# Two-layer mixture-of-experts transformer, float32: each piece of expert weights loaded, awaited and given back as two halves

## The chip, the core and the metric

The kernel runs on one core of a Trainium2 chip. The core has TensorE (PE, with PEld for its weight loads), VectorE (DVE), ScalarE (ACT), GpSimd (POOL) and SyncE (SP), which here only issues transfers, and 16 DMA engines that bring data from DRAM. The metric is the device time of the launch in microseconds; lower is better.

## The reference

The function is a stack of two models; the second one's layers (RWKV, long convolution, neighbourhood attention, convolutional FFN) aren't touched by the change. The first has two layers of gated MLP and attention, cross attention to a memory, and a mixture of experts over 512 tokens of width 1024:

```python
def expert_choice_moe(h, w_router, w_gate, w_up, w_down):
    cap = EC_FACTOR * s // N_EXPERTS            # 2 * 512 // 16 = 64 tokens for each expert
    logits = jnp.einsum('bsd,de->bse', h, w_router, preferred_element_type=jnp.float32)
    aff = jax.nn.softmax(logits, axis=-1)
    gates, idx = lax.top_k(aff.transpose(0, 2, 1), cap)
    xs = h[b_ix, idx]
    a = jnp.einsum('becd,edf->becf', xs, w_gate)      # w_gate, w_up, w_down: [2, 16, 1024, 1024]
    u = jnp.einsum('becd,edf->becf', xs, w_up)
    y = jnp.einsum('becf,efd->becd', jax.nn.silu(a) * u, w_down)
    y = y * gates[..., None].astype(y.dtype)
    return jnp.zeros_like(h).at[b_ix, idx].add(y)
```

## The kernel before

The program is a row of stages, one after the other; each starts when all engines have left the one before. All large weights pass through a ring (class `Ring`). They are cut on the host into pieces of 128 partitions x 4096 floats, 16 KB a partition and 2 MB in all, laid out in DRAM in the order of use. The ring has 2 slots of its own, 2 more during the first model, and 3 lent ones (`lent_weights`) during the experts: 7 slots in an experts stage.

Only SP moves pieces. `feed` walks through the list of pieces in order. For each it picks the slot whose last piece is the oldest, waits until the semaphore `weights_used` says that this piece has been used (line 94), and issues one transfer (line 95). The user calls `take` ahead of a piece, which waits for the slot's `weights_landed` semaphore, and `done` on its last instruction, which adds 1 to `weights_used`.

The change is in the stage that `Experts.run` builds. First the tokens are routed (softmax, largest 64 of each expert, places), with little work for TensorE. Then follows a loop over 16 experts with 6 pieces each: two of `w_gate`, two of `w_up`, two of `w_down`, each with 4 blocks of 128 rows by 1024 columns. Per expert TensorE runs, in this order: `project(GATE, 0)`, `spread_places`, `project(GATE, 1)`, `put_back(0)` of the expert before, `project(UP, 0)`, `put_back(1)`, `project(UP, 1)`, `put_back(2)`, `turn_hidden`, `put_back(3)`, `down(0)`, up to three `pick`s for the next group of 4 experts, `down(1)`. A `project` or `down` uses one piece in 8 matmuls (4 blocks, two halves of the columns); each counts twice in the trace, so a piece is x16 there. ACT and DVE wait on `weights_used` too, to know that a projection is complete (`piece(e, 1)`, `piece(e, 3)`, `piece(e, 5)`).

When the stage begins, 4 pieces are loaded, and SP at once fills the 3 lent slots. So 7 pieces of 96 are there before the first matmul of an expert, and 89 are refills: each waits until the piece 7 places before it has been used. Behind the last expert piece, `feed` goes on with `w_in` of the next layer.

Of the kernel before, what the change touches and what calls it, by code (L numbers as in the profile page):

```python
# [26 lines left out]
P = 128  # L27
T = 512
D = 1024
# [21 lines left out]
class Ring:  # L51


    def __init__(self, nc, ctx, pieces, slots, lent):
        tile = ctx.enter_context(nc.sbuf_tensor("weight_ring", [P, slots, KT * SLOT_COLS], F32))
        self.landed = [ctx.enter_context(nc.semaphore(f"weights_landed{i}")) for i in range(slots + lent)]
        self.used = ctx.enter_context(nc.semaphore("weights_used"))
        self.begun = ctx.enter_context(nc.semaphore("first_weights_landed"))
        self.pieces, self.own = pieces, slots
        self.tiles = [tile[:, i, :] for i in range(slots)] + [None] * lent  # L60
# [13 lines left out]
    def begin(self, sp, cols):  # L74

        src, n = self.pieces[0]
        to, src = (a.rearrange("p (k n) -> p k n", n=n)[:, :, cols] for a in (self.tiles[0][:, 0:src.shape[1]], src))
        if cols.start == 0:
            sp.dma_start(to, src).then_inc(self.begun, 16)
        else:  # L80
            sp.dma_start(to, src).then_inc(self.landed[0], 16)
            self.last[0], self.slot[0], self.fills[0], self.fill[0], self.issued = 0, 0, 1, 1, 1

    def feed(self, sp, n):

        self.fed += n
        while self.issued < len(self.pieces):
            i = self.issued
            s = min((s for s in range(len(self.tiles)) if i < self.until[s]), key=lambda s: self.last[s])
            if self.last[s] >= self.fed:  # L90
                break
            if self.last[s] >= 0:
                sp.wait_ge(self.used, self.last[s] + 1)
            src, _ = self.pieces[i]
            sp.dma_start(self.tiles[s][:, 0:src.shape[1]], src).then_inc(self.landed[s], 16)
            self.last[s], self.slot[i] = i, s
            self.fills[s] += 1
            self.fill[i] = self.fills[s]
            self.issued += 1
# [10 lines left out]

    def view(self, i):

        src, cols = self.pieces[i]
        return self.tiles[self.slot[i]][:, 0:src.shape[1]].rearrange("p (k n) -> p k n", n=cols)

    def done(self, ins):

        ins.then_inc(self.used, 1)

# [41 lines left out]
def col_pieces(flat, rows, cols, tall=KT * P, wide=SLOT_COLS):  # L161
# [3 lines left out]
    for _, h, _, n in piece_shapes(rows, cols, tall, wide):  # L165
        out.append((flat[at:at + h * n].rearrange("(p x) -> p x", p=P), n))
# [64 lines left out]
class Chain:  # L231
# [369 lines left out]
    def tensor(self, pe):  # L601
# [10 lines left out]
        def product(unit, ks, finish):  # L612
            job = unit.job

            def weights_here(m):
# [9 lines left out]
                if unit.ends_piece:  # L625
                    pe.wait_ge(self.ring.used, unit.piece + 1)
# [734 lines left out]
class Experts:  # L1361
# [80 lines left out]
    def run(self):  # L1442
# [4 lines left out]
        with ExitStack() as ctx:  # L1447
# [30 lines left out]
            piece = lambda e, j: first + 6 * e + j + 1  # L1478
# [18 lines left out]
            def _(pe):  # L1497
# [51 lines left out]
                def down(e, part):  # L1549
# [5 lines left out]
                    for k in range(4):  # L1555
                        for half in range(2):
# [76 lines left out]
            def _(act):  # L1633
# [11 lines left out]
                for e in range(NE):  # L1645
# [3 lines left out]
                    act.wait_ge(ring.used, piece(e, 1))  # L1649
# [3 lines left out]
                    act.wait_ge(ring.used, piece(e, 5))  # L1653
# [3 lines left out]
            def _(dve):  # L1657
# [74 lines left out]
                for e in range(NE):  # L1732
# [10 lines left out]
                    dve.wait_ge(ring.used, piece(e, 3))  # L1743
# [1454 lines left out]
def weight_pieces(dram):  # L3198

    out = []  # L3200
    for l in range(2):
# [5 lines left out]
        for e in range(N_EXPERTS):  # L3207
            for w in ("w_gate", "w_up", "w_down"):
                out += col_pieces(dram[w][l, e], D, D, tall=D // 2, wide=D)
# [183 lines left out]
```

## Time and profile before

| | us |
|---|---|
| median of 3 runs | 3629.76 (3628.56 to 3632.1) |
| profiled execution, its time | 3630.33 |
| profiled execution, its span | 3629.0 |
| TensorE busy | 3366.4, 93% of the span |
| VectorE busy | 1816.6, 50% |
| ScalarE busy | 1110.0, 31% |
| bytes read from DRAM | 589.91 MB, 163 GB/s over the span |
| mean granted TensorE clock | 0.965 |

The two experts stages lie at about 437 to 931 and 1362 to 1858 us. A busy TensorE is a modelled figure; what matters for the change is which engine waits for which inside those stages, and when in them.

### The profile page before, as it was taken

Reading aid. Unit: us, or ns where it says so; the run is one execution under the profiler, and the core shown is the slowest. Engines: PE = TensorE matmul, PEld = TensorE weight load, DVE = VectorE, ACT = ScalarE, POOL = GpSimd, SP = SyncE. Lnnn points to the kernel's source line nnn. Section 1 sums busy time; section 2 is a strip of 40 time slices with the busy share of each in tenths; the row PEclk is TensorE's granted clock in tenths of the full one; section 3 lists DMA queues with packets and bytes.
Section 4 is the critical chain, followed back from the end, with each engine's and each line's share of the span. In section 5 each row is a group of like instructions: output and inputs, shape, how many; then the busy total and the mean of one; then the engine's idle time right before and its main releaser. Section 6 shows DMA issues by size and latency. Waiting matters only on the chain. (4 is left out here: it accounts for less than half of the span.)

```text
span 3629.0 us, 55850 instructions
## 1 busy us (share of the span) xinstructions
PE 3366.4 (93%) x23850; PEld 2342.4 (65%) x23850; DVE 1816.6 (50%) x2872; ACT 1110.0 (31%) x1871; POOL 252.6 (7%) x208
## 2 busy tenths in 40 slices
PE   8889789999888997999989788889999999899999
PEld 7587543333667753333358687857888878688887
DVE  3655433222466443222245666566665462766635
ACT  3543300000345331000032333224333432643323
POOL 1011000000101100000020222201000110010001
PEclk9899999999989998999999899999999999999999
DMA  5031379999402217999952000012222222122222
GB/s 219 13 116 70 117 308 428 427 427 428 194 36 94 93 47 294 427 427 428 428 236 105 2 3 3 3 36 91 101 93 87 99 93 82 59 100 93 93 84 79
DMA packets 51798, 595.59 MB, mean 164 GB/s; under 512 B 5472, under 2 KB 9824, under 8 KB 16224
## 3 DMA queue, kind: packets, MB, share of 16 engines
q1 hardware_dynamic: 51552, 592.03, 40.5%
q8 instruction: 189, 3.10, 0.3%
q14 instruction: 57, 0.47, 0.0%
HBM read 589.91 MB, written 2.10 MB: 163 GB/s over the span
## 5 line engine op out<-in xcount | busy, mean ns | idle before, releaser
L648 PE MATMUL psum<-source_hi,weights_hi 128*128 128x512 f32 (+1 forms) x2352 | 921.4, 392 | 43.9 <-DVE weights_lo L535 35.7
L648 PE MATMUL psum<-source_lo,weights_hi 128*128 128x512 f32 (+1 forms) x2352 | 910.3, 387 | 0.0
L648 PE MATMUL psum<-source_hi,weights_lo 128*128 128x512 f32 (+1 forms) x2352 | 910.1, 387 | 0.0
L648 PEld LDWEIGHTS psum<-source_hi,weights_hi 128*128 128x128 f32 x2352 | 448.7, 191 | 144.7 <-DVE weights_lo L535 44.5
L648 PEld LDWEIGHTS psum<-source_lo,weights_hi 128*128 128x128 f32 x2352 | 448.8, 191 | 89.8 <-issue 2.9
L648 PEld LDWEIGHTS psum<-source_hi,weights_lo 128*128 128x128 f32 x2352 | 448.1, 191 | 88.8
L535 DVE TENSOR_TENSOR weights_lo<-weight_ring,weights_hi 128x1024 fp32r<-128x1024 f32 (+4 forms) x304 | 340.7, 1126 | 302.0 <-ACT weights_hi L483 301.3
L483 ACT CAST weights_hi<-weight_ring 128x1024 fp32r<-128x1024 f32 (+4 forms) x304 | 289.6, 960 | 660.2 <-PE psum L648 649.4
L1690 DVE TENSOR_TENSOR x<-psum,x 128x512 f32<-128x512 f32 x256 | 164.3, 685 | 199.7 <-PE psum L1571 199.7
L597 POOL TENSOR_TENSOR sums_of_squares<-squares 128x512 f32<-128x512 f32 (+1 forms) x17 | 27.2, 1598 | 2524.4 <-ACT squares L503 2524.4
L1538 PE MATMUL psum<-lent_weights,branches 128*64 128x512 f32 x800 | 182.1, 597 | 2.5 <-DMA lent_weights<-in_w_gate 2.5
L1538 PE MATMUL psum<-weight_ring,branches 128*64 128x512 f32 x624 | 141.8, 597 | 2.5 <-DMA weight_ring<-in_w_up 1.9
L1538 PE MATMUL psum<-weight_ring_first,branches 128*64 128x512 f32 x624 | 141.8, 597 | 2.5 <-DMA weight_ring_first<-in_w_up 2.3
L1538 PEld LDWEIGHTS psum<-lent_weights,branches 128*64 128x64 f32 x800 | 54.0, 137 | 114.6 <-issue 110.4
L597 POOL TENSOR_TENSOR sums_of_squares<-sums_of_squares,squares 128x512 f32<-128x512 f32 (+1 forms) x86 | 118.7, 1380 | 133.0 <-ACT squares L503 127.8
L2505 DVE TENSOR_TENSOR before_convolution<-psum,roots 128x512 f32<-128x512 f32 x100 | 69.0, 690 | 109.1 <-PE psum L648 109.0
L648 PE MATMUL psum<-weights_hi,source_hi 128*128 128x256 f32 x384 | 110.6, 288 | 11.7 <-DVE weights_lo L535 11.7
L2177 PE MATMUL psum<-rwkv_scratch 64*64 64x64 f32 x3584 | 108.2, 218 | 9.2 <-PEq L138 6.9
L2177 PEld LDWEIGHTS psum<-rwkv_scratch 64*64 64x64 f32 x3584 | 106.2, 135 | 15.0 <-issue 10.4
L1557 PE MATMUL psum<-lent_weights,hidden_t 128*64 128x512 f32 x480 | 109.1, 598 | 2.8 <-ACT hidden_t L1652 1.3
L1136 DVE TENSOR_TENSOR x<-psum,x 128x512 f32<-128x512 f32 x64 | 44.2, 691 | 132.8 <-PE psum L648 132.6
L1652 ACT COPY hidden_t<-psum 128x512 f32<-128x512 f32 x32 | 18.8, 587 | 298.9 <-PE psum L1546 298.9
(380 smaller groups left out, 4661.9 us busy)
## 6 DMA issues: line engine op xcount, KB each, us to landing
lent_weights<-in_w_down SPq DMA_DIRECT2D x30, 2048.0 KB, 17.9
lent_weights<-in_w_gate SPq DMA_DIRECT2D x26, 2048.0 KB, 16.6
lent_weights<-in_w_up SPq DMA_DIRECT2D x24, 2048.0 KB, 18.8
weight_ring<-in_ffn_w_up SPq DMA_DIRECT2D x22, 2048.0 KB, 7.7
weight_ring<-in_w_up SPq DMA_DIRECT2D x20, 2048.0 KB, 17.6
weight_ring_first<-in_w_up SPq DMA_DIRECT2D x20, 2048.0 KB, 17.3
weight_ring_first<-in_w_gate SPq DMA_DIRECT2D x19, 2048.0 KB, 16.5
weight_ring<-in_w_gate SPq DMA_DIRECT2D x19, 2048.0 KB, 16.5
```

Source lines behind the costliest of these rows:

```text
L483: act.copy(self.whi[:, ks, unit.slot * P:unit.slot * P + unit.cols], self.ring.view(unit.piece)[:, ks, unit.c0:unit.c0 + unit.cols])\
L535: ins = dve.tensor_tensor(lo, self.ring.view(unit.piece)[:, ks, unit.c0:unit.c0 + unit.cols], hi.bitcast(F32), ALU.subtract)
L597: pool.tensor_tensor(total, square(q) if m == 1 else total, square(q + m), ALU.add).then_inc(self.added, 1)
L648: ins = pe.matmul(ps, a, b, start=k == 0 and q == 0, stop=k == job.rows // P - 1 and q == 2)
L1136: return dict(evac=lambda i, dve, ps, link, r: dve.tensor_tensor(K.x[:, i, :], ps, K.x[:, i, :], ALU.add), engine=lambda i: "dve")
L1538: ins = pe.matmul(psum[HALF * half:HALF * half + HALF, which, :], self.xs[:, k, e // GROUP % 2, e % GROUP * CAP:(e % GROUP + 1) * CAP], w[ ...
L1557: ins = pe.matmul(psum[HALF * half:HALF * half + HALF, self.ROWS, :], hid_t[:, k, part * HALF:(part + 1) * HALF], w[:, k, half * 512:half ...
L1652: act.copy(hid_t[:, :, :], psum[:, self.TURN, :].rearrange("p (j s) -> p j s", j=4)).then_inc(hid_t_kept, 1)
L1690: dve.tensor_tensor(x, psum[:, bank(), :], x, ALU.add).then_inc(misc_free, 1)
L2177: ins = pe.matmul(K.psum[r, bank + d, c], w[d][r, lhs, c], w[d][r, rhs, c], start=True, stop=True)
L2505: return dve.tensor_tensor(self.raw[:, m % 3, :], ps, r[0], ALU.mult)
```

## The change

Every expert piece is marked with `ExpertPiece(True)`. SP moves such a piece as two transfers: the first two of its four blocks (8 KB of each partition's 16 KB), then the other two. The first half has the old semaphore `weights_landed`, the second a new one, `second_half_landed`. The first transfer waits only until the first half of the slot's old piece has been used, the second until all of it has. TensorE calls `done` after the fourth of a piece's 8 matmuls as well as after the last, and waits for the second half after the fourth. `weights_used` thus counts 2 for an expert piece and 1 for any other, and `releases[i]` is its value when piece i is used up; ACT, DVE and the other stages wait for these values at the same places in the work as before. Pieces of other weights are moved whole.

```diff
@@ Ring.__init__
+        self.second_landed = [ctx.enter_context(nc.semaphore(f"second_half_landed{i}")) for i in range(slots + lent)]
+        self.releases, n = [], 0
+        for _, _, experts in pieces:
+            n += 2 if experts else 1
+            self.releases.append(n)
@@ Ring.feed
-            if self.last[s] >= 0:
-                sp.wait_ge(self.used, self.last[s] + 1)
-            src, _ = self.pieces[i]
-            sp.dma_start(self.tiles[s][:, 0:src.shape[1]], src).then_inc(self.landed[s], 16)
+            src, _, experts = self.pieces[i]
+            old = self.last[s]
+            if experts and experts.in_halves:
+                half = src.shape[1] // 2
+                if old >= 0:
+                    sp.wait_ge(self.used, self.releases[old] - 1 if self.pieces[old][2] else self.releases[old])
+                sp.dma_start(self.tiles[s][:, 0:half], src[:, 0:half]).then_inc(self.landed[s], 16)
+                if old >= 0:
+                    sp.wait_ge(self.used, self.releases[old])
+                sp.dma_start(self.tiles[s][:, half:2 * half], src[:, half:2 * half]).then_inc(self.second_landed[s], 16)
+                self.second_fills[s] += 1
+                self.second_fill[i] = self.second_fills[s]
+            else:
+                if old >= 0:
+                    sp.wait_ge(self.used, self.releases[old])
+                sp.dma_start(self.tiles[s][:, 0:src.shape[1]], src).then_inc(self.landed[s], 16)
@@ Ring
+    def take_second_half(self, eng):
+        i = self.taken - 1
+        if i in self.second_fill:
+            eng.wait_ge(self.second_landed[self.slot[i]], 16 * self.second_fill[i])
@@ Experts.run
-            piece = lambda e, j: first + 6 * e + j + 1
+            used_up = lambda e, j: ring.releases[first + 6 * e + j]
@@ project
                     for k in range(4 * part, 4 * part + 4):
+                        if k % 4 == 2:
+                            ring.done(ins)
+                            ring.take_second_half(pe)
@@ down
                     for k in range(4):
+                        if k == 2:
+                            ring.done(ins)
+                            ring.take_second_half(pe)
```

On SP, the place is the start of the stage's refills; each row is one transfer with its shape, and `weights_used` is what TensorE raises. Before:

```order
50 L95 DMA weight_ring_first<-in_w_gate 128x4096 [waits weights_used]
51 L95 DMA weight_ring_first<-in_w_up 128x4096 [waits weights_used]
52 L95 DMA weight_ring<-in_w_up 128x4096 [waits weights_used]
53 L95 DMA weight_ring<-in_w_down 128x4096 [waits weights_used]
54 L95 DMA lent_weights<-in_w_down 128x4096 [waits weights_used]
```

With the change:

```order
60 L106 DMA weight_ring_first<-in_w_gate 128x2048 [waits weights_used]
61 L109 DMA weight_ring_first<-in_w_gate 128x2048 [waits weights_used]
62 L106 DMA weight_ring_first<-in_w_up 128x2048 [waits weights_used]
63 L109 DMA weight_ring_first<-in_w_up 128x2048 [waits weights_used]
64 L106 DMA weight_ring<-in_w_up 128x2048 [waits weights_used]
65 L109 DMA weight_ring<-in_w_up 128x2048 [waits weights_used]
```

Each transfer has become two, each behind a wait of its own; their order and their slots are the same.

On TensorE, the place is the first two pieces of the first expert, with the spread of the places between them. Before:

```order
1730 L1538 MATMUL psum<-weight_ring_first,branches 64x512 [waits weights_landed2,misc_free]
1731 L1538 MATMUL psum<-weight_ring_first,branches 64x512 x7
1732 L1530 MATMUL psum<-place_rows,constants 128x512 [waits misc_free]
1733 L1538 MATMUL psum<-weight_ring_first,branches 64x512 [waits weights_landed3]
1734 L1538 MATMUL psum<-weight_ring_first,branches 64x512 x7
```

With the change:

```order
1730 L1574 MATMUL psum<-weight_ring_first,branches 64x512 [waits weights_landed2,misc_free]
1731 L1574 MATMUL psum<-weight_ring_first,branches 64x512 x3
1732 L1574 MATMUL psum<-weight_ring_first,branches 64x512 [waits second_half_landed2]
1733 L1574 MATMUL psum<-weight_ring_first,branches 64x512 x3
1734 L1563 MATMUL psum<-place_rows,constants 128x512 [waits misc_free]
1735 L1574 MATMUL psum<-weight_ring_first,branches 64x512 [waits weights_landed3]
1736 L1574 MATMUL psum<-weight_ring_first,branches 64x512 x3
1737 L1574 MATMUL psum<-weight_ring_first,branches 64x512 [waits second_half_landed3]
```

The matmuls are the same and in the same order; a wait for the second half now stands ahead of the fifth of each piece's eight.

## Rows read from the trace of the kernel before

**Rows 1.** The page, part 2: GB/s of the DMA engines in 40 equal slices
```profile
GB/s 219 13 116 70 117 308 428 427 427 428 194 36 94 93 47 294 427 427 428 428 236 105 2 3 3 3 36 91 101 93 87 99 93 82 59 100 93 93 84 79
```

**Rows 2.** Windows in layer 0's experts; last three columns: clock, DMA share, GB/s
```profile
455.00:477.00 22.00, 15.70 (x149) 12.96 (x149) 9.89 (x21) 0.00 (x0) 0.00 (x0) 0.75 0.00 1
700.00:800.00 100.00, 99.18 (x482) 36.99 (x480) 29.95 (x50) 6.86 (x11) 0.00 (x0) 1.00 1.01 427
```

**Rows 3.** Waits of PE for DMA, 437 to 940: us in total, times, longest
```profile
PE psum L1538 <- DMA weight_ring<-in_w_up: 1.3, 3, 0.6
...
PE psum L1538 <- DMA weight_ring_first<-in_w_gate: 0.2, 1, 0.2
```

**Rows 4.** Timeline of PE, end of layer 0's experts: start us, us, engine, what
```profile
875.23 3.65 PE L1538 MATMUL psum<-weight_ring,branches 128*64 128x512 f32 x16 [0.15 <-DMA weight_ring<-in_w_up]
...
894.84 3.65 PE L1538 MATMUL psum<-lent_weights,branches 128*64 128x512 f32 x16 [1.23 <-DMA lent_weights<-in_w_gate]
899.74 3.65 PE L1538 MATMUL psum<-weight_ring_first,branches 128*64 128x512 f32 x16 [0.19 <-DMA weight_ring_first<-in_w_gate]
...
919.76 3.65 PE L1557 MATMUL psum<-lent_weights,hidden_t 128*64 128x512 f32 x16 [0.66 <-DMA lent_weights<-in_w_down]
```

**Rows 5.** Timeline of PE and SP, start of layer 0's experts: start us, us
```profile
473.38 3.63 PE L1538 MATMUL psum<-weight_ring_first,branches 128*64 128x512 f32 x16
...
477.06 0.33 SPq L95 DMA_DIRECT2D weight_ring_first<-in_w_gate  x1
481.69 0.33 SPq L95 DMA_DIRECT2D weight_ring_first<-in_w_up  x1
```

**Rows 6.** Timeline of PE's weight loads at a piece boundary
```profile
642.24 0.14 PEld L1557 LDWEIGHTS psum<-weight_ring_first,hidden_t 128*64 128x64 f32 x2 [0.29 <-issue]
642.67 0.14 PEld L1538 LDWEIGHTS psum<-weight_ring_first,branches 128*64 128x64 f32 x2 [0.29 <-issue]
```

**Rows 7.** DMA issues at 477.06, 481.69 and 883.86: KB each, us to landing
```profile
weight_ring_first<-in_w_gate SPq DMA_DIRECT2D x1, 2048.0 KB, 7.6
...
weight_ring_first<-in_w_up SPq DMA_DIRECT2D x1, 2048.0 KB, 9.3
...
weight_ring<-in_w_down SPq DMA_DIRECT2D x1, 2048.0 KB, 31.0
```

**Rows 8.** Timeline of ACT where the next stage begins
```profile
931.90 0.39 ACT L483 CAST weights_hi<-weight_ring_first 128x256 fp32r<-128x256 f32 x1
```

**Rows 9.** SP's issues (start us, us) and landings, 2048 KB then 1024 KB
```profile
913.23 6.24 SPq L95 DMA_DIRECT2D weight_ring<-in_w_in  x2
...
weight_ring<-in_w_in SPq DMA_DIRECT2D x1, 2048.0 KB, 21.2
...
weight_ring<-in_w_in SPq DMA_DIRECT2D x1, 1024.0 KB, 17.7
...
9.31 0.91 SPq L95 DMA_DIRECT2D weight_ring_first<-in_w_in  x2
...
weight_ring_first<-in_w_in SPq DMA_DIRECT2D x1, 2048.0 KB, 18.4
...
weight_ring_first<-in_w_in SPq DMA_DIRECT2D x1, 1024.0 KB, 20.5
```

**Rows 10.** SP's first issues, then their landings (x first, x last, w_in)
```profile
3.13 3.40 SPq L3162 DMA_DIRECT2D x<-in_x  x7
...
5.88 0.65 SPq L3162 DMA_DIRECT2D x<-in_x  x1
...
6.57 0.57 SPq L81 DMA_DIRECT2D weight_ring<-in_w_in  x1
...
x<-in_x SPq DMA_DIRECT2D x1, 256.0 KB, 5.0
...
x<-in_x SPq DMA_DIRECT2D x1, 256.0 KB, 6.3
...
weight_ring<-in_w_in SPq DMA_DIRECT2D x1, 1536.0 KB, 9.8
```

More of the change, by code:

```diff
@@ L12 @@
 import math
+from dataclasses import dataclass
 from contextlib import ExitStack, contextmanager
@@ L58, in __init__ @@
         self.begun = ctx.enter_context(nc.semaphore("first_weights_landed"))
+        self.second_landed = [ctx.enter_context(nc.semaphore(f"second_half_landed{i}")) for i in range(slots + lent)]
         self.pieces, self.own = pieces, slots
+        self.releases, n = [], 0
+        for _, _, experts in pieces:
+            n += 2 if experts else 1
+            self.releases.append(n)
+        self.second_fills = [0] * (slots + lent)
+        self.second_fill = {}
         self.tiles = [tile[:, i, :] for i in range(slots)] + [None] * lent
@@ L74, in begin @@
     def begin(self, sp, cols):
-        src, n = self.pieces[0]
+        src, n, _ = self.pieces[0]
         to, src = (a.rearrange("p (k n) -> p k n", n=n)[:, :, cols] for a in (self.tiles[0][:, 0:src.shape[1]], src))
@@ L109, in take @@
         return self.view(i)
+    def take_second_half(self, eng):
+        i = self.taken - 1
+        if i in self.second_fill:
+            eng.wait_ge(self.second_landed[self.slot[i]], 16 * self.second_fill[i])
     def view(self, i):
-        src, cols = self.pieces[i]
+        src, cols, _ = self.pieces[i]
         return self.tiles[self.slot[i]][:, 0:src.shape[1]].rearrange("p (k n) -> p k n", n=cols)
@@ L118, in done @@
         ins.then_inc(self.used, 1)
+@dataclass
+class ExpertPiece:
+    in_halves: bool
 class Core:
@@ L165, in col_pieces @@
     for _, h, _, n in piece_shapes(rows, cols, tall, wide):
-        out.append((flat[at:at + h * n].rearrange("(p x) -> p x", p=P), n))
+        out.append((flat[at:at + h * n].rearrange("(p x) -> p x", p=P), n, None))
         at += h * n
@@ L625, in weights_here @@
                 if unit.ends_piece:
-                    pe.wait_ge(self.ring.used, unit.piece + 1)
+                    pe.wait_ge(self.ring.used, self.ring.releases[unit.piece])
                 else:
@@ L1648, in _ @@
                         act.wait_ge(misc_free, scaled[c])
-                    act.wait_ge(ring.used, piece(e, 1))
+                    act.wait_ge(ring.used, used_up(e, 1))
                     act.activation(gated[:, :], psum[:, self.GATE, :], ACT.Silu, scale=column(e, 0)).then_inc(gate_kept, 1)
@@ L1652, in _ @@
                     act.copy(hid_t[:, :, :], psum[:, self.TURN, :].rearrange("p (j s) -> p j s", j=4)).then_inc(hid_t_kept, 1)
-                    act.wait_ge(ring.used, piece(e, 5))
+                    act.wait_ge(ring.used, used_up(e, 5))
                     act.copy(y_hi[:, :], psum[:, self.ROWS, :]).then_inc(y_hi_kept, 1)
@@ L1742, in _ @@
                     dve.wait_ge(gate_kept, e + 1)
-                    dve.wait_ge(ring.used, piece(e, 3))
+                    dve.wait_ge(ring.used, used_up(e, 3))
                     dve.scalar_tensor_tensor(out=hid[:, :], in0=psum[:, self.UP, :], scalar=column(e, 1), in1=gated[:, :],
@@ L3207, in weight_pieces @@
         for e in range(N_EXPERTS):
-            for w in ("w_gate", "w_up", "w_down"):
-                out += col_pieces(dram[w][l, e], D, D, tall=D // 2, wide=D)
+            six = [p for w in ("w_gate", "w_up", "w_down") for p in col_pieces(dram[w][l, e], D, D, tall=D // 2, wide=D)]
+            out += [(src, n, ExpertPiece(True)) for i, (src, n, _) in enumerate(six)]
     first, out = out, []
```

## The prediction, made before the change was run

> **What bounds the kernel now.** I read the page first: its slices of DMA have two plateaus near 428 GB/s [rows 1]. Those are the experts of the two layers, and the change touches nothing else. So I cut layer 0's stage into windows [rows 2] and take layer 1, whose plateau looks the same, to be alike. From 455 to 477 us the DMA engines idle: the ring's 7 slots are full, and TensorE releases none while the tokens are routed. In mid-stage DMA stands at 1.01 with TensorE at 99%.
>
> With both near full, the question is which of them sets the end. The list of waits answers: TensorE waits for weights only 4.2 us in the whole stage of layer 0, in five rows of which the first and the last stand here [rows 3]. In order of time [rows 4] all of it lies at the end. The first such wait is before the piece at 875.23; later pieces start at 894.84 and 899.74, 4.90 us apart, each behind its transfer, after matmuls of 3.65 us and a wait. So TensorE consumes a little faster than DMA delivers, lives on the 7 pieces' lead for 400 us, and has used it up at 875. From there the transfers decide, and since DMA has run full since the refills began [rows 1, 2], the end is: start of the refill stream, plus 89 pieces' transfers, plus TensorE's work behind the last landing.
>
> **The sum.** Three terms for each layer.
>
> Start. The first refill is issued at 477.06, when the first piece's last matmul has ended [rows 5]. The piece began at 473.38 [rows 5]. Weight loads come in steps of 0.43 us [rows 6], two records a step and 16 a piece, so half a piece is four steps, 1.72 us. The first half's slot is given back that much earlier, and an idle DMA can begin on it. Half a transfer (some 2.45 us) then covers the time to the second release. Gain 1.72. The later early releases gain nothing: late in the stage a transfer lands 31.0 us after its issue [rows 7], so six pieces queue in front of DMA, and a shorter time in a slot only lengthens the queue.
>
> End. The last piece starts at 919.76, when it has landed, and all that follows hangs on it, up to the next stage's first weights, cast at 931.90 [rows 4, 8]. With halves, the first four steps run while the second half is still arriving (2.45 us of transfer against 1.72 of work), and only 1.72 remains behind the landing. Gain 1.72. TensorE is free in time for this: it was idle 0.66 us before that piece. Together 3.44 a layer, less than the 4.2 that the waits hold, so TensorE's own work does not cap it.
>
> The transfers. What lands stays the same in bytes, but 128 rows of 16 KB become 256 rows of 8 KB, each half a strided read. The trace has no queue of such halves in this stage. It does have 1024 KB transfers behind 2048 KB ones: the one issued at 919.14 lands 2.41 us after its predecessor (919.14 + 17.7 less 913.23 + 21.2), the one issued at 9.79 lands 2.58 after (9.79 + 20.5 less 9.31 + 18.4) [rows 9]. Twice that is 4.82 to 5.16 against 4.90: from nothing to 0.26 us a piece. Shorter rows narrow it. Seven x tiles of 128 rows x 2 KB land between 3.13 + 5.0 and 5.88 + 6.3, six steps of 0.675 us, 84 ns for each of an engine's eight rows [rows 10]. At the expert rate (4.90 us for eight rows of 16 KB, 612 ns each) 2 KB would take 77, so a row costs 8 ns beyond its bytes. The transfer of 1536 KB in rows of 1536 B that skip 512 B each lands 4.19 us after the last x tile (6.57 + 9.8 less 12.18), 65 ns for each of 64 rows where bytes alone make 57: again 8 ns, so skipping in DRAM adds nothing [rows 10]. Eight more rows an engine make 0.064 us a piece. I take 0.05, a little under it, because the later of the two 1024 KB steps, the one in the same full stream, shows none. Over the 88 landings behind the first that is 4.4 us a layer.
>
> The Trainium skill, page "DMA: Bandwidth & Descriptors", section "Why small descriptors are slow (HBM only)", puts the overhead at some three cycles a packet; by the 32-byte beats of that section a piece in halves would take 0.6% longer, an estimate of 0.03 us, and the sum would come out at -1.9 us for both layers. The rows' 8 ns decide here.
>
> At nothing I put the rest. SP issues 192 more transfers, 0.33 us each [rows 5]: two in 4.90 us, and SP has nothing else queued. The waiting half on SP holds back only the next piece's request, which stands behind six queued pieces anyway. On TensorE each piece gets one more wait and one more signal. The boundary between two pieces without work between them has both already, and the 0.43 us step runs through it, from 642.24 to 642.67 [rows 6]; its upper bound is then 0.02 us a piece, 2 us a layer, hidden behind DMA's lead as long as it stays under the 4.2 us. ACT and DVE wait for the same end of the same pieces. w_in's third piece lands at 913.23 + 21.2 = 934.4, so its first, two transfers earlier, at 924.6, and that is first cast at 931.90 [rows 8, 9]: 7.3 us of cover, of which the net delay takes less than 3.
>
> Sum: (4.4 - 3.44) x 2 = +1.9 us on the profiled execution's 3630.3, 3632.2. That execution lies 0.6 over the median of the runs, so 3631.6 for the median. The change does what it says, and the engine that would profit was not short of lead until the end.
>
> **The rivals.** A measurement of this kernel can tell about 0.2%, 7.3 us, from no change.
>
> *The stream keeps its rate and starts better.* For it: the step of 2.41 us. The row cost would then be zero, and -3.44 x 2 = -6.9. In addition the second refill lands 6.3 us behind the first (481.69 + 9.3 less 477.06 + 7.6) where 4.90 are due [rows 5, 7]: DMA loses 1.4 us as it wakes. If half-size requests spare that too in both layers, the sum is -9.7, 3621. Against it: the wake-up is likely paid by the first packets whatever their size. It needs both parts to pass 7.3. Chance 0.12.
>
> *Halves cost more than rows say (slower).* Place: every landing from 484 to 920. It turns the sum over 7.3 us when a piece takes 0.080 us longer: 88 x 0.080 = 7.1 less 3.44, twice. At the upper row bound, 0.26, the sum is (22.9 - 3.44) x 2 = +38.9, 3669. For it: the step of 2.58 us, and that no row shows a long queue of halves. Against it: the 8 ns a row, which two row lengths, contiguous and not, give alike. Chance 0.17.
>
> The section "Anatomy of one DMA — SWDGE (gpsimd) path" of the Trainium skill's page "DMA: Bandwidth & Descriptors" gives each transfer a fixed 2 us next to its bytes. Here the row shows 4.90 us from landing to landing against 7.6 for the first, which found the queue empty [rows 7], so a fixed part exists and is hidden by the queue.
>
> *The fixed part is not hidden for halves.* If the 2.7 us between 7.6 and 4.90 stood between landings even in part, a tenth of it would give 88 x 0.27 = 23.8 less 3.44 a layer, +40.6 in all, 3671. Nothing in the rows shows it. Chance 0.03.
>
> *The extra waits on TensorE break its stream.* If a wait cost 0.1 us, 96 of them outweigh the 4.2 us of slack: TensorE would bound, about +9.6 - 4.2 = +5.4 a layer, 3641. Against it: the boundary in [rows 6]. Chance 0.05.
>
> **How the numbers follow.** The forecast and its near variants, row costs of 0 to 0.08 us a piece without a spared wake-up, run from -6.9 to +7.2 us, all within 0.2%: 0.63. Faster: 0.12. Slower: 0.17 + 0.03 + 0.05 = 0.25. The range leaves out the unlikely part of the first rival and the upper part of the second: from 3623 (no row cost, 3630 - 6.9) to 3645 (0.12 us a piece, (10.6 - 3.44) x 2 = +14.3), which holds about 0.85.
>
> **What the profile after would show.** The first refill issued near 475.3 instead of 477.1. 1024 KB transfers that land every 2.45 to 2.50 us in a DMA share of 1.00 to 1.01, and a rate of 423 to 425 GB/s where it was 427. The stage's first wait for DMA some 50 to 100 us earlier than 875, more and smaller waits in sum, half of them at the middle of pieces. 1.7 us from the last landing to the end of the matmuls. The rest of the kernel unchanged. I am wrong if the rate falls under 420 GB/s, if the weight loads' 0.43 us step breaks in the middle of pieces before 700, or if the wake-up loss is gone.

## The result, and the profile after

The median was 3628.32 us before and 3633.60 us after, 20 runs each (3622.5 to 3638.13, and 3631.13 to 3639.23). The ratio is 1.0016 with a 95% interval of 1.0010 to 1.0022: the change costs 5.8 us (3.6 to 8.0). That is a real loss and a small one, under the 0.2% (7.3 us) from which the prediction counts a kernel as slower. The prediction was 3631.6 us in a range of 3623 to 3645, and a loss of 1.9 us.

The profiled execution took 3631.13 us, its span 3629.7. First the page, part 2, as in [rows 1]:

```profile
GB/s 219 13 116 70 117 312 421 421 421 421 215 35 94 93 47 300 421 421 421 421 248 96 19 4 3 4 36 78 109 98 88 99 93 82 58 100 93 93 84 79
```

Both plateaus fell from 427 or 428 to 421 GB/s. They still are plateaus: the windows answering to [rows 2] show full DMA engines and a full TensorE.

```profile
455.00:477.00 22.00, 16.09 (x150) 13.11 (x150) 9.51 (x21) 0.00 (x0) 0.00 (x0) 0.76 0.06 13
700.00:800.00 100.00, 99.18 (x480) 36.98 (x478) 30.47 (x51) 6.85 (x11) 0.00 (x0) 1.00 1.01 421
```

So the DMA engines are as busy as before (1.01) and move less. Next the start of layer 0's experts, the timeline of TensorE and SP and the landings of these three transfers, as in [rows 5] and [rows 7]:

```profile
472.90 3.63 PE L1574 MATMUL psum<-weight_ring_first,branches 128*64 128x512 f32 x16
...
474.85 0.33 SPq L106 DMA_DIRECT2D weight_ring_first<-in_w_gate  x1
476.57 0.33 SPq L109 DMA_DIRECT2D weight_ring_first<-in_w_gate  x1
479.49 0.33 SPq L106 DMA_DIRECT2D weight_ring_first<-in_w_up  x1
...
weight_ring_first<-in_w_gate SPq DMA_DIRECT2D x1, 1024.0 KB, 4.9
...
weight_ring_first<-in_w_gate SPq DMA_DIRECT2D x1, 1024.0 KB, 6.7
...
weight_ring_first<-in_w_up SPq DMA_DIRECT2D x1, 1024.0 KB, 7.8
```

The first refill now starts 1.95 us after the first expert matmul (474.85 less 472.90), where it was 3.68: the stream starts 1.73 us earlier. But the first half lands at 479.75, the second at 483.27 and the third at 487.29, steps of 3.5 and 4.0 where a full stream makes 2.5.

The stage's end, on TensorE, as in [rows 4]:

```profile
866.69 1.94 PE L1574 MATMUL psum<-weight_ring_first,branches 128*64 128x512 f32 x8 [0.54 <-DMA weight_ring_first<-in_w_gate]
...
915.21 1.94 PE L1574 MATMUL psum<-weight_ring,branches 128*64 128x512 f32 x8 [0.49 <-DMA weight_ring<-in_w_up]
...
919.41 3.65 PE L1596 MATMUL psum<-weight_ring,hidden_t 128*64 128x512 f32 x16
922.89 1.89 PE L1596 MATMUL psum<-lent_weights,hidden_t 128*64 128x512 f32 x8
925.13 1.94 PE L1596 MATMUL psum<-lent_weights,hidden_t 128*64 128x512 f32 x8 [0.35 <-DMA lent_weights<-in_w_down]
```

A piece is now x8 and x8 wherever TensorE stopped in its middle. The last wait ends at 925.13, and 1.94 us of matmuls are left behind it, where a whole piece of 3.65 was left before. The first wait for DMA comes at 866.69 instead of 875.23. All waits of TensorE for DMA in the stage, the groups that answer to [rows 3]:

```profile
PE psum L1574 <- DMA weight_ring<-in_w_up: 2.8, 3, 1.8
...
PE psum L1574 <- DMA lent_weights<-in_w_gate: 1.1, 2, 0.6
PE psum L1574 <- DMA weight_ring_first<-in_w_gate: 1.1, 2, 0.6
PE psum L1596 <- DMA lent_weights<-in_w_down: 0.7, 2, 0.4
...
PE psum L1574 <- DMA weight_ring_first<-in_w_up: 0.5, 1, 0.5
```

They sum to 6.2 us in ten waits, where the five rows before summed to 4.2.

From the first expert matmul to the end of the last, layer 0 takes 454.17 us (472.90 to 925.13 + 1.94) against 450.03 before (473.38 to 919.76 + 3.65). Layer 1, read in the same way, takes 454.76 against 450.31. The stages cost 8.6 us in this pair of profiles. Yet the two spans differ by 0.7 us, so the rest of the kernel was 7.9 us faster in this one execution. Two windows show where, the stretch between the two expert stages and the stretch behind the second, of before:

```profile
923.40:1361.90 438.50, 394.34 (x2145) 306.03 (x2144) 230.97 (x382) 185.74 (x345) 43.42 (x36) 0.94 0.21 80
1848.60:3629.00 1780.40, 1671.42 (x14754) 1380.77 (x14754) 1061.31 (x1603) 668.12 (x1061) 165.47 (x127) 0.97 0.19 70
```

And of after:

```profile
927.10:1361.35 434.25, 388.62 (x2143) 301.71 (x2144) 230.86 (x382) 185.55 (x345) 43.42 (x36) 0.96 0.22 82
1852.60:3629.70 1777.10, 1666.08 (x14754) 1377.74 (x14754) 1061.27 (x1603) 668.08 (x1061) 165.32 (x127) 0.97 0.19 71
```

The same instructions, 4.25 and 3.30 us less (7.6 of the 7.9), and in the first stretch a mean granted clock of 0.96 instead of 0.94. The change touches nothing there. One profile of each kernel would have told that the change costs nothing; the 20 runs of each say otherwise. The experiments below are therefore read twice, by their timed ratio and by the length of the experts stages, and the rest is checked by profiling both kernels again.

### The profile page after: what moved, and what is told of

It is laid out like the page before. It is cut to its first block and busy times, and to the rows that moved or that the text cites. A ratio compares the mean times of both kernels' runs of the same rounds, so it can differ in the third digit from the quotient of the medians.

```text
span 3629.7 us, 56042 instructions
## 1 busy us (share of the span) xinstructions
PE 3358.6 (93%) x23850; PEld 2333.0 (64%) x23850; DVE 1816.8 (50%) x2872; ACT 1109.7 (31%) x1871; POOL 252.4 (7%) x208
## 5 line engine op out<-in xcount | busy, mean ns | idle before, releaser
L681 PE MATMUL psum<-source_lo,weights_hi 128*128 128x512 f32 (+1 forms) x2352 | 908.6, 386 | 0.0
L1691 ACT COPY hidden_t<-psum 128x512 f32<-128x512 f32 x32 | 18.8, 587 | 302.0 <-PE psum L1582 302.0
## 6 DMA issues: line engine op xcount, KB each, us to landing
lent_weights<-in_w_down SPq DMA_DIRECT2D x60, 1024.0 KB, 19.4
```

The source lines that it names most:

```text
L681: ins = pe.matmul(ps, a, b, start=k == 0 and q == 0, stop=k == job.rows // P - 1 and q == 2)
L1691: act.copy(hid_t[:, :, :], psum[:, self.TURN, :].rearrange("p (j s) -> p j s", j=4)).then_inc(hid_t_kept, 1)
```

## The experiments

The theory at the outset (A): the price is the row. A 2 MB piece in 256 rows of 8 KB takes longer than in 128 rows of 16 KB, whoever issues it. Rivals: (B) the price is the transfer, with its own completion; (C) it is the stride, since a half skips the other half in DRAM; and, for the start and the end, that what the halves give back is not the sum of an early release and an early arrival. Each timed kernel shares its chip and its runs of the kernel before with those of its group. The last column is the length of the two experts stages, each from its first expert matmul to the end of its last, in sum and in one profile; the kernel before has 900.8 us there and the change 908.6, each as the mean of two profiles. The diffs show the lines that decide; lines that mark the pieces, lay them out or count fills are left out.

| kernel | median us | kernel before there | ratio (95%) | difference | experts stages us |
|---|---|---|---|---|---|
| rows8k_one_transfer | 3643.21 | 3629.83 | 1.0039 (1.0026 to 1.0051) | +13.4 | 913.4 (+12.6) |
| rows16k_two_transfers | 4478.36 | 3629.83 | 1.2337 (1.2321 to 1.2354) | +848.5 | not read |
| halves_contiguous | 3635.81 | 3629.83 | 1.0016 (1.0007 to 1.0025) | +6.0 | 907.2 (+6.4) |
| quarters | 3654.36 | 3629.83 | 1.0068 (1.0055 to 1.0080) | +24.5 | 931.2 (+30.4) |
| arrive_in_halves | 3637.65 | 3629.47 | 1.0022 (1.0012 to 1.0031) | +8.2 | 909.8 (+8.9) |
| released_in_halves | 3638.51 | 3629.47 | 1.0027 (1.0016 to 1.0039) | +9.0 | 912.8 (+12.0) |
| ends_in_halves | 3623.08 | 3629.47 | 0.9982 (0.9973 to 0.9991) | -6.4 | 898.4 (-2.4) |
| ends_in_quarters | 3620.39 | 3629.47 | 0.9979 (0.9970 to 0.9987) | -9.1 | 898.3 (-2.6) |
| last_expert_in_halves | 3623.00 | 3629.60 | 0.9983 (0.9975 to 0.9992) | -6.6 | 896.4 (-4.4) |

The ratio is not the quotient of the two medians; the column beside it is the difference of the medians, and the rougher of the two. Where the text below gives a time, it is the ratio's.

### Rows of 8 KB, one transfer, no halves

The kernel before, with each expert piece laid out as 2 x 128 rows of 8 KB and still moved by one transfer:

```diff
-            sp.dma_start(self.tiles[s][:, 0:src.shape[1]], src).then_inc(self.landed[s], 16)
+            sp.dma_start(self.tiles[s][:, :].rearrange("p (h x) -> p h x", h=2), self.short_rows[i]).then_inc(self.landed[s], 16)
```

> The kernel before, with every expert piece still one transfer, awaited and given back whole, but laid out in DRAM so that it is read as 256 contiguous rows of 8 KB and not 128 of 16 KB. It has none of the change's gains. Theory A (the price of the halves is paid for each row): pieces land every 4.97 us in the full stream, as with the change (2 x 2.485), 0.075 more than before; 88 x 0.075 x 2 layers = 13 us slower than before. Theory B (it is paid for each transfer and its semaphore writes): 4.90 us, time as before. Theory C (it comes from reading halves with a stride in DRAM): 4.90 us and time as before too.

It is 1.0039, +14 us (9 to 19): the whole price of the rows, which was to be 13, with none of the gains. A window of its steady stream:

```profile
600.00:700.00 100.00, 98.56 (x538) 38.55 (x536) 29.05 (x47) 6.16 (x10) 0.00 (x0) 1.00 1.01 421
```

And the same window of after:

```profile
600.00:700.00 100.00, 98.56 (x538) 38.60 (x536) 29.05 (x47) 6.16 (x10) 0.00 (x0) 1.00 1.01 421
```

One transfer with one completion gives the same 421 GB/s as two with two. The landings say it more finely. From the third refill on, the median step from one piece's landing to the next is 4.894 us in the kernel before, 4.970 in after and 4.970 here. Yet the trace has 640 packets of under 512 B, which are the completions, in these 100 us of after, and 321 here. So the second transfer, its semaphore and its wait cost DMA nothing that can be seen, and theory B falls.

### Rows of 16 KB, two transfers

The other half of the test, 64 partitions a transfer, so that rows keep their 16 KB:

```diff
+                for rows in (slice(0, HALF), slice(HALF, P)):
+                    sp.dma_start(self.tiles[s][rows, 0:src.shape[1]], src[rows, :]).then_inc((self.landed if rows.start == 0 else self.others_landed)[s], 16)
```

> The kernel before, with every expert piece split by partitions: two transfers of 64 rows of 16 KB, both issued when the old piece is used up, both awaited ahead of the piece. As many transfers as with the change, but the rows are as long as before. Theory A (price for each row): a piece lands every 4.90 us, time as before. Theory B (price for each transfer): 4.97 us a piece, 13 us slower than before. Theory C (stride): 4.90, as before.

Neither theory had this. The window and its DMA queue:

```profile
600.00:700.00 100.00, 65.37 (x289) 24.23 (x286) 15.32 (x26) 3.13 (x5) 0.00 (x0) 0.84 1.01 215
```

DMA is full by its share, 1.01, and moves 215 GB/s, half of 427. Each 16 KB row takes about twice the time, 1.23 us in the mean of its packets where it was 0.62. As a test of B this run says nothing, since what it pays is the price of 64 partitions. The Trainium skill, page "SBUF — State Buffer", section "Can I just issue two DMAs to hit both halves?", has the rule that a single transfer's span of partitions picks its ports, and that two transfers can't be fused; the 215 GB/s agree with it.

### Halves that are contiguous in DRAM

The change, with the layout of the first experiment, so that each half is 1 MB without a gap:

```diff
-                sp.dma_start(self.tiles[s][:, 0:half], src[:, 0:half]).then_inc(self.landed[s], 16)
+                sp.dma_start(self.tiles[s][:, 0:half], experts.halves[:, 0, :]).then_inc(self.landed[s], 16)
```

> The changed kernel, with the two halves of each expert piece laid out apart in DRAM, so that each 1024 KB transfer reads one contiguous block instead of 8 KB of every 16 KB. Theories A and B (rows or transfers): halves still land every 2.485 us, time as with the change, about 6 us slower than before. Theory C (stride): 2.45 us, and the time falls by 88 x 0.075 x 2 = 13 us, to 7 us under the kernel before.

The window:

```profile
600.00:700.00 100.00, 98.56 (x540) 38.64 (x538) 30.34 (x49) 6.17 (x10) 0.00 (x0) 1.00 1.01 421
```

Again 421 GB/s, a median step of 4.970 and 4.972 us in the two layers, and a ratio of 1.0016, that of the change itself. The stride has no price that shows; theory C falls.

### Quarters

The change with four transfers, four waits and four releases a piece:

```diff
+                for q in range(4):
+                    if old >= 0:
+                        sp.wait_ge(self.used, self.releases[old] - (3 - q if self.pieces[old][2] else 0))
+                    sp.dma_start(self.tiles[s][:, q * part:(q + 1) * part], src[:, q * part:(q + 1) * part])
@@ project
-                        if k % 4 == 2:
+                        if k % 4:
                             ring.done(ins)
-                            ring.take_second_half(pe)
+                            ring.take_quarter(pe, k % 4)
```

> The changed kernel with quarters for halves: each expert piece moves as four transfers of 128 rows x 4 KB, and TensorE awaits and gives back each quarter by itself. Theories A and B (a fixed price for each further row or transfer): three times the price of the halves, 0.225 us, so a piece lands every 5.12 us; the gains at the two ends grow from 1.72 to 2.58 us each; (88 x 0.225 - 5.16) x 2 = 29 us slower than before. If the price were paid once for any piece that is not moved whole: 4.97 us a piece, (6.6 - 5.16) x 2 = 3 us slower than before. If TensorE's extra waits cost anything, its weight loads' step of 0.43 us would break after each pair of matmuls.

The window, and the queue in the same stretch (packets, MB, share of the 16 engines):

```profile
600.00:700.00 100.00, 98.56 (x538) 38.67 (x538) 30.34 (x49) 6.16 (x10) 0.00 (x0) 1.00 1.03 409
...
q1 hardware_dynamic: 11210, 40.82, 102.4%
```

Rows of 4 KB run at 409 GB/s. TensorE does the same matmuls in the same time (98.56 us busy), with four waits for a piece where the kernel before has one; so its waits show no cost either. If the price counts rows, it should triple from halves to quarters, 24 added rows an engine instead of 8, and it does: the median step is 5.120 us, 0.226 over that of the kernel before, against 0.076 for halves. The experts stages grew by 30.4 us, as the expected 29 wants. The timed loss, +25 us (20 to 29), is nearer the lower side; this difference comes back below.

### Half of the gains each

The change without the early release, so that both halves wait for the whole old piece:

```diff
-                    sp.wait_ge(self.used, self.releases[old] - 1 if self.pieces[old][2] else self.releases[old])
+                    sp.wait_ge(self.used, self.releases[old])
```

> The changed kernel, but SP issues both halves of a piece only when the whole old piece has been used; TensorE still awaits each half by itself. This keeps the gain at the stage's end (1.72 us) and drops the one at its start. By the sum with the measured price of the rows: (6.6 - 1.72) x 2 = 9.8 us slower than before, with the first refill issued at the end of the first piece again (some 1.7 us later against its start than with the change), and 1.7 us from the last landing to the end of the matmuls. Rival (the early release costs DMA more at its wake-up than it gives): the time is that of the changed kernel or less, +6 us.

And the change without the early arrival, so that TensorE waits for both halves ahead of a piece (the same in `down`):

```diff
                     w = ring.take(pe)
+                    ring.take_second_half(pe)
                     for k in range(4 * part, 4 * part + 4):
                         if k % 4 == 2:
                             ring.done(ins)
-                            ring.take_second_half(pe)
```

> The changed kernel, but TensorE awaits both halves ahead of the piece; it still gives each back by itself. This keeps the gain at the start and drops the one at the end: 3.4 us from the last landing to the end of the matmuls, (6.6 - 1.72) x 2 = 9.8 us slower than before. Rival (the halves' arrival one by one is of no use at the end, because ACT and DVE hide it): time as with the change, +6 us.

The first: TensorE and SP at the start, and the last piece.

```profile
474.49 3.63 PE L1574 MATMUL psum<-weight_ring_first,branches 128*64 128x512 f32 x16
...
478.16 0.33 SPq L106 DMA_DIRECT2D weight_ring_first<-in_w_gate  x1
...
927.36 1.94 PE L1596 MATMUL psum<-lent_weights,hidden_t 128*64 128x512 f32 x8 [0.35 <-DMA lent_weights<-in_w_down]
```

The second:

```profile
476.45 3.63 PE L1574 MATMUL psum<-weight_ring_first,branches 128*64 128x512 f32 x16
...
478.41 0.33 SPq L106 DMA_DIRECT2D weight_ring_first<-in_w_gate  x1
...
929.50 3.65 PE L1596 MATMUL psum<-lent_weights,hidden_t 128*64 128x512 f32 x16 [0.43 <-DMA lent_weights<-in_w_down]
```

In the place where it arises, one gain goes in each and the other stays. Without the early release the first refill is back at 3.67 us behind the first matmul (478.16 less 474.49), and 1.94 us are left behind the last wait. Without the early arrival the first refill still comes 1.96 us behind it (478.41 less 476.45), but TensorE waits ahead of the last piece until 929.50, with all of it to do.

The times do not separate the two from the change: +8.0 us (4.4 to 11.3) and +9.8 (5.8 to 14.2) against +5.8 (3.6 to 8.0). The experts stages say more. Without the early arrival they are 4.3 us longer than with the change, both layers together, where 3.4 was due. Without the early release they are only 1.2 us longer. The refills began 1.7 us later in each layer, but from the first issue to the last landing they took 449.2 us where the change takes 450.4. So of the early release's 1.72 us only some 0.6 reached the end of a stage here, which speaks for the rival, that the early release costs DMA at its wake-up. It is not shown: this is one profile, the same number scatters by up to 1.4 us among the four layers of the change, and halves_contiguous, which has the early release, took 449.7.

### Halves only where they pay

If the rows cost and only the two ends gain, then halves for two of 96 pieces, the first refill and the last piece, should keep the gain and drop the price:

```diff
-            out += [(src, n, ExpertPiece(True)) for i, (src, n, _) in enumerate(six)]
+            out += [(src, n, ExpertPiece((e, i) in ((1, 1), (N_EXPERTS - 1, 5)))) for i, (src, n, _) in enumerate(six)]
```

> The changed kernel, but only two of a layer's 96 pieces move in halves: the first refill (w_gate of expert 1, second piece) and the last piece of the stage. All others move whole, in rows of 16 KB. If the price lies in the rows of all 89 refills and the gains only at the two ends, the price shrinks to 2 x 0.075 = 0.15 us a layer and the gains stay: (0.15 - 3.44) x 2 = 6.6 us faster than before. Rival (halving the first refill makes DMA lose more as it wakes, 1 us of it in layer 0 with the change): 4 us faster. Rival (the gains are smaller than worked out, and the change cost only what its rows did not explain): no difference from before.

The same with quarters for these two:

> As the kernel with only the first refill and the last piece in halves, but with those two in quarters, and every expert piece given back in four steps. Gains of 2.58 us at each end: (0.45 - 5.16) x 2 = 9.4 us faster than before. Rival (a third and a fourth signal and wait a piece, or the wake-up in still smaller requests, eat the further gain): as with halves, 4 to 7 us faster.

0.9982 and 0.9979, -6.5 us (-9.8 to -3.3) and -7.6 us (-10.9 to -4.7): both beat both kernels, and quarters are not told from halves. But in their profiles the experts stages were only 2.4 and 2.6 us shorter than before, in sum, less than the intervals of the times allow. Where the rest was gained, no run shows (see the end of the next section). So -6.5 against the expected -6.6 does not bear that sum out. The last pieces of ends_in_halves on TensorE read:

```profile
909.57 3.65 PE L1574 MATMUL psum<-weight_ring,branches 128*64 128x512 f32 x16 [0.57 <-DMA weight_ring<-in_w_up]
...
915.47 3.65 PE L1596 MATMUL psum<-weight_ring,hidden_t 128*64 128x512 f32 x16
918.96 3.60 PE L1596 MATMUL psum<-lent_weights,hidden_t 128*64 128x512 f32 x16
```

There is no wait in the last piece at all. TensorE came to it late, because it had waited for the whole of the last `w_up` piece until 909.57 and everything behind that piece is a chain of its own work. Its end gain is 0.5 us: 3.17 us from the last landing to the end of the matmuls, where the kernel before has 3.70 and the change 1.98. So the end gain needs halves in the pieces ahead of the last, too. Hence a third version:

```diff
+            out += [(src, n, ExpertPiece((e, i) == (1, 1) or e == N_EXPERTS - 1)) for i, (src, n, _) in enumerate(six)]
```

> As the kernel with only the first refill and the last piece in halves, but with all six pieces of the last expert in halves. With the last piece alone in halves, 3.17 us still lay between its landing and the last matmul's end in layer 0, where the change left 1.98: TensorE was then late from the piece before, which it had awaited whole. Theory: with the last expert in halves this falls to 1.98 in both layers, and five more pieces cost 5 x 0.075 = 0.4 us a layer, so a net gain of 0.8 us a layer beside the kernel with two pieces in halves, 6 to 8 us faster than before in all. Rival (the 3.17 come from something else, such as the transfer of w_in behind the last piece): still 3.17.

```profile
908.65 1.94 PE L1574 MATMUL psum<-weight_ring,branches 128*64 128x512 f32 x8 [1.64 <-DMA weight_ring<-in_w_up]
...
916.33 1.89 PE L1596 MATMUL psum<-lent_weights,hidden_t 128*64 128x512 f32 x8
918.60 1.94 PE L1596 MATMUL psum<-lent_weights,hidden_t 128*64 128x512 f32 x8 [0.38 <-DMA lent_weights<-in_w_down]
```

Here the last piece waits in its middle again and 1.94 us are left behind the last landing. The experts stages are 2.0 us shorter in sum than in ends_in_halves, 1.0 a layer where 0.8 was expected. The timed ratio, 0.9983 (0.9975 to 0.9992), does not separate the three versions from each other; it separates all of them from the kernel before.

### Both kernels profiled again

> The kernel before, profiled once more. Its first profile spent 450.0 and 450.3 us from the first to the last matmul of the two experts stages, 438.5 us between them and 1780.4 behind them, at a granted clock of 0.94 between them; the changed kernel's spent 454.2 and 454.8, 434.3 and 1777.1, at 0.96. Theory (stretches outside the experts differ by chance, with the stretches of half clock): experts again within 1 us of 450, the other two stretches elsewhere within some 3 us. Rival (the halves also quicken what follows the experts, by the clock): 438 and 1780 again.

> The changed kernel, profiled once more. Theory (chance outside the experts): 454 to 455 us in each experts stage again, the stretches between and behind them 2 to 4 us from 434.3 and 1777.1 in either direction. Rival (the halves quicken what follows): 434 and 1777 again, both below those of the kernel before.

They took 3630.43 and 3634.46 us. The stretches between and behind the experts stages, of the kernel before:

```profile
928.31:1362.12 433.81, 389.07 (x2143) 301.33 (x2144) 231.07 (x382) 185.64 (x345) 43.47 (x36) 0.96 0.21 81
1848.83:3629.10 1780.27, 1669.02 (x14754) 1377.86 (x14754) 1061.30 (x1603) 668.77 (x1061) 165.53 (x127) 0.97 0.20 70
```

And of after:

```profile
929.01:1362.72 433.71, 390.92 (x2143) 303.30 (x2144) 230.98 (x382) 185.49 (x345) 43.43 (x36) 0.95 0.22 82
1852.58:3633.10 1780.52, 1671.69 (x14755) 1380.94 (x14754) 1061.21 (x1603) 667.94 (x1061) 165.42 (x127) 0.97 0.20 71
```

The first stretch takes 433.7 to 433.8 us in both kernels this time, the second 1780.3 and 1780.5. So the 7.6 us by which after was faster there in the first pair did not come back, and they belong to the executions and not to the change, at least for the most part. The experts stages, by contrast, repeat: 900.3 and 901.4 us in sum before, 908.9 and 908.2 after. Single layers missed what was expected of them by little, 451.1 us in one of before and 453.4 in one of after.

A small share of the change outside the experts stages is not ruled out. The mean granted clock of a whole launch was 0.9664 in the 58 timed runs of the kernel before that stand beside the experiments; among these, a run with 0.001 more was some 1.4 us shorter. It was 0.9675 in the 20 runs of the change, 0.9686 in quarters, 0.9674 in ends_in_halves and 0.9688 in ends_in_quarters. The timed differences of these last three lie 4 to 6 us below those of their experts stages, and a higher clock goes that way. But it was 0.9677 in arrive_in_halves, whose two differences agree within 1 us, and 0.9658 in halves_contiguous. No run isolates this.

## Why the prediction held, and which term was mis-sized

The time was met within 2.0 us, the loss less well: 1.9 us was forecast, outside the measured 3.6 to 8.0. Part of the agreement is luck, since the kernel before was 1.4 us faster in the median of the 20 runs than in that of the three that the forecast started from. The mechanism and the signs held; one term was too small.

**What bounds the kernel: right.** The transfers decide the end of the stage. TensorE's work is the same 98.56 us from 600 to 700 us in after, with one transfer, with contiguous halves and with quarters, while the stages lengthen with the rows (900.8, then 907 to 913, then 931 us).

**Start, 1.72 us: the size right, the reason only in part.** The first refill came 1.73 us earlier behind the first matmul, and 3.67 behind it again when only the early release was taken away. The third refill landed 23.0 us behind the first matmul before and 21.6 after (means of four layers), a gain of 1.7 once the rows' 0.2 are added. But without the early release it landed at 22.1: most of the gain was there already, since the stream started faster behind two halves issued together. That is one profile, in a number that scatters by 1.1 us in the kernel before.

**End, 1.72 us: right,** 3.65 against 1.94 left behind the last wait. But its reason, "TensorE is free in time for this: it was idle 0.66 us before that piece", would have given 0.66 at most, since TensorE could begin the last piece only that much earlier. The full gain rests on the pieces ahead of the last also being awaited by halves; ends_in_halves, without them, got 0.5.

**The transfers, 0.05 us a piece: the mis-sized term.** In the prediction's words, "I take 0.05, a little under it, because the later of the two 1024 KB steps, the one in the same full stream, shows none." The stream itself says more. Two `lent_weights` pieces of before, 84 pieces apart (issue and landing each):

```profile
494.48 0.33 SPq L95 DMA_DIRECT2D lent_weights<-in_w_down  x1
889.77 0.33 SPq L95 DMA_DIRECT2D lent_weights<-in_w_down  x1
...
lent_weights<-in_w_down SPq DMA_DIRECT2D x1, 2048.0 KB, 11.2
lent_weights<-in_w_down SPq DMA_DIRECT2D x1, 2048.0 KB, 29.9
```

That is (919.67 - 505.68) / 84 = 4.929 us a piece. The second half of the same piece after:

```profile
493.99 0.33 SPq L109 DMA_DIRECT2D lent_weights<-in_w_down  x1
...
lent_weights<-in_w_down SPq DMA_DIRECT2D x1, 1024.0 KB, 10.7
```

It landed at 504.69, and the last half at 925.1, where TensorE's last wait ended: 420.4 / 84 = 5.005. The price is 0.076 us a piece, as the median steps give it too (4.970 less 4.894), and 88 x 0.076 = 6.7 a layer instead of 4.4. With it the sum is (6.7 - 3.44) x 2 = +6.5 us, inside the measured 3.6 to 8.0. In quarters the median step is 0.226 us longer than before, for 24 added rows an engine: 9.4 ns a row, where the 8 added by halves make 9.5. The rows of the profile had said 8 ns, 0.064 us, and I shaded that down on the strength of one step of 2.41 us, which stood between two transfers of different kinds. One step between two landings rounded to a tenth can't carry a hundredth of a microsecond; a mean over many can.

The Trainium skill, page "DMA: Bandwidth & Descriptors", section "Why small descriptors are slow (HBM only)", has some three cycles a packet. The 0.03 us estimated from it falls short of the 0.076 measured by more than half; the measurement decides.

**The wake-up, a rival's part: not spared.** In layer 0 before, the second refill lost 1.4 us. After, the steps of 3.5 and 4.0 us lose 1.0 and 1.5. Over two profiles of each kernel and both layers, the third refill landed 19.4 us behind the first one's issue before (18.8 to 19.9) and 19.7 after (19.1 to 20.5); of the 0.3 the rows are 0.2. From the first issue to the last landing it was 443.05 us and 450.36, 7.3 more, of which 6.7 is the rows. Most of the other 0.6 lies behind the third piece, in single steps 1 to 2 us longer than the rest, which every kernel has and one layer of after had more of. With 7.3 the sum is (7.3 - 3.44) x 2 = +7.7 us, and the four profiles show the experts stages at 900.8 and 908.6 in the mean, +7.7. The 20 runs of each say 5.8, and their interval just holds that.

**At nothing: right.** A second transfer, a second completion, a stride, a wait and a signal more on TensorE: no run shows a price. TensorE's weight loads kept their step in the middle of a piece. In the timeline of after, the fourth and the fifth load of a piece (two records each), one on either side of its new wait:

```profile
643.46 0.14 PEld L1574 LDWEIGHTS psum<-weight_ring_first,branches 128*64 128x64 f32 x2 [0.29 <-issue]
643.89 0.14 PEld L1574 LDWEIGHTS psum<-weight_ring_first,branches 128*64 128x64 f32 x2 [0.29 <-issue]
```

They are 0.43 us apart, like the others of the piece. The 0.33 us that the prediction gives SP for each issue did not hold late in the stage (2.1 us, last section), and cost nothing. w_in's cover held; the next stage's first cast, on ACT:

```profile
935.28 0.39 ACT L516 CAST weights_hi<-weight_ring_first 128x256 fp32r<-128x256 f32 x1
```

It stands 462.4 us behind the first expert matmul, where it was 458.5 [rows 5, 8]. The 3.9 us between them is what layer 0's stage lost (4.1) within 0.3 us.

**Wrong details.** The rate was to be 423 to 425 GB/s and is 421, which is the mis-sized price again. The first wait was to come 50 to 100 us earlier and came 9 us earlier (866.69). I had set the slower stream against TensorE's lead and left out two things that add to it: the stream begins 1.7 us earlier, and TensorE needs only the first half of a piece to go on. That reading is argued from the rows and no run isolates it.

**The rivals.** "The stream keeps its rate and starts better" fell on both parts for the change. The stream started better in two other kernels, the third refill 18.4 us behind the first issue in arrive_in_halves and 18.6 in halves_contiguous (19.7 after), in one profile each. "Halves cost more than rows say" had the right direction and decided from 0.080 us a piece; at 0.076 the change stops just short of it, and "slower" was nearer than its chance of 0.17 tells. "The fixed part is not hidden" and "the extra waits break TensorE's stream" fell: one transfer and two gave 421 GB/s and a step of 4.970 us, and the step in quarters grew by the row price and nothing beside it.

## What to carry to other kernels

In a stream of transfers that fills the DMA engines, what a split costs is its rows: here each added row cost some 9.5 ns on its engine, from 16 to 8 KB and from 8 to 4 KB, while more transfers, more completions and strides showed no price. What a split gains, it gains once at each end of the stream; so split the first refill and the last few pieces, and leave those between whole. The change for all 96 pieces lost 5.8 us; for two pieces it won 6.5 (3.3 to 9.8), though the experts stages account for only 2.4 of it. And when an effect is of a few microseconds in thousands, read it in the stage that it is in and time the kernels many times; in one pair of profiles, code that was the same differed by 7.9 us.

## What the runs showed of the hardware that I had not expected

Transfers to 64 partitions run at half the rate, 215 GB/s for 427, at a full share of the DMA engines (1.01).

The first transfers of a stream that finds DMA idle lose time beyond the first one's own: 1.4 us in the second piece before (2.4 in layer 1), 2.5 us in the next two halves after. What it is that they wait for, no run shows.

Late in the stage SP takes much longer to issue. Two rows of SP's timeline of after, beside the 0.33 us at the stage's start:

```profile
895.67 2.14 SPq L106 DMA_DIRECT2D lent_weights<-in_w_down  x1
897.85 2.13 SPq L109 DMA_DIRECT2D lent_weights<-in_w_down  x1
```

2.1 us an issue, when transfers land 27 us after it and ten of 1 MB are outstanding; with up to eight an issue took 0.33 us. It fits the rows that are outstanding better than their bytes or the transfers: in quarters an issue took 1.1 us from eleven outstanding on, in rows8k_one_transfer 2.8 us with six, and in the kernel before 0.33 with six expert pieces. The slow issues had 1280, 1408 and 1536 rows ahead of them, the quick ones of the kernel before 768. No run isolates this either. SP has nothing else to do here, and the queue behind it is long, so it costs nothing; what it would cost a kernel whose SP serves several streams, no run shows.
